# Four landing places for weight tiles and three more rows for gathered experts in a two-block transformer kernel

## What is computed

```python
# first block, last step: retrieval of single-neuron experts, 128 of them for each token
q = (xt @ w_query).reshape(t, PEER_HEADS, 2, PEER_KEY_DIM // 2)
s = jnp.einsum('thkd,hknd->thkn', q, sub_keys)
vals, idx = lax.top_k(s, PEER_TOPK)
cand = (vals[:, :, 0, :, None] + vals[:, :, 1, None, :]).reshape(t, PEER_HEADS, PEER_TOPK * PEER_TOPK)
best, pos = lax.top_k(cand, PEER_TOPK)
expert = i1 * N_SUB_KEYS + i2            # taken from idx at pos
gate = jax.nn.softmax(best, axis=-1)
a = jnp.einsum('cd,ced->ce', xb, u_tab[eb])
w = gb * jax.nn.gelu(a)
out = jnp.einsum('ce,ced->cd', w, v_tab[eb])
# second block, each of two layers
x = x + 0.5 * swiglu(rms_norm_2(x, ffn1_norm[l]), ffn1_w13[l], ffn1_w2[l])
x = x + (three gated attention branches) @ w_out[l]
x = x + 0.5 * swiglu(rms_norm_2(x, ffn2_norm[l]), ffn2_w13[l], ffn2_w2[l])
```

## Time and profile before

| | us |
|---|---|
| median of 3 runs | 4303.13 |
| lowest and highest | 4300.82, 4307.96 |
| the profiled execution | 4305.1 |
| its span, first to last instruction | 4303.3 |
| PE busy in the span | 3993.2 (93%) |
| POOL busy | 2348.1 (55%) |
| DVE busy | 2181.4 (51%) |
| ACT busy | 1402.0 (33%) |

### The profile page before, as it was taken

The page is one execution under the profiler, slowest core; times in us unless marked ns, Lnnn a source line. Parts: engine busy times, 40 slices in busy tenths (PEclk is TensorE's granted clock), DMA queues, the critical chain, the costliest instruction groups (busy, mean ns, idle before and its releaser), DMA issues.

```text
span 4303.3 us, 50720 instructions
## 1 busy us (share of the span) xinstructions
PE 3993.2 (93%) x17008; PEld 2839.7 (66%) x17008; DVE 2181.4 (51%) x4308; ACT 1402.0 (33%) x3024; POOL 2348.1 (55%) x3124
## 2 busy tenths in 40 slices
PE   9999988787887888988999999999999999999998
PEld 7877633333333555577867767888888867768887
DVE  8376877767776665543154544331332165534322
ACT  3142332222223444443223433332332133323222
POOL 7646543333334556656655456665665745546654
PEclk9999999999999999999999999999999999999999
DMA  5242899999999999944322212323223312213232
GB/s 148 86 106 79 349 427 427 427 427 427 427 412 387 394 369 367 411 134 132 98 69 74 64 60 83 103 96 99 94 97 95 98 54 69 77 49 108 94 97 82
DMA packets 187403, 828.07 MB, mean 192 GB/s; under 512 B 41360, under 2 KB 44096, under 8 KB 121664
## 3 DMA queue, kind: packets, MB, share of 16 engines
q0 software_dynamic: 73728, 536.90, 30.0%
q1 hardware_dynamic: 88448, 281.93, 20.6%
q10 hardware_dynamic: 25024, 6.69, 0.8%
HBM read 819.94 MB, written 4.59 MB: 192 GB/s over the span
## 4 chain that ended last, share of the span: by engine, by line
PE 67%; DMA 14%; DVE 9%; POOL 3%; issue 3%; ACT 2%; DVEq 1%; ACTq 0%; SPq 0%; POOLq 0%
PE bank L891 17%; PE bank L893 16%; PE bank L892 16%; PE bank L1290 7%; DMA rows_o<-in_peer_uv,of_picks_int 5%; DMA rows_x<-in_peer_uv,of_picks_int 3%; POOL wl L731 3%; DMA rows_w<-in_peer_uv,of_picks_int 2%; DMA raw<-in_w_l 2%; PE bank L985 1%; DVE rows_o L2696 1%; DMA work<-in_peer_uv,of_picks_int 1%; DVE rows_x L2696 1%; PE bank L1385 1%; PE bank L1517 1%
## 5 line engine op out<-in xcount | busy, mean ns | idle before, releaser
L731 POOL TENSOR_TENSOR wl<-raw,wh 128x256 fp32r<-128x256 f32 (+1 forms) x2064 | 1598.3, 805 | 598.0 <-ACT wh L1977 561.9
L891 PE MATMUL bank<-xh,wh 128*128 128x512 f32 (+1 forms) x2304 | 885.3, 384 | 27.8 <-POOL wl L731 27.0
L893 PE MATMUL bank<-xh,wl 128*128 128x512 f32 (+1 forms) x2304 | 863.9, 375 | 0.0
L892 PE MATMUL bank<-xl,wh 128*128 128x512 f32 (+1 forms) x2304 | 863.3, 375 | 0.0
L1977 ACT ACTIVATE wh<-raw 128x1024 fp32r<-128x1024 f32 x296 | 312.3, 1057 | 703.2 <-PE bank L893 491.2
L891 PEld LDWEIGHTS bank<-xh,wh 128*128 128x128 f32 x2304 | 435.4, 189 | 148.4 <-issue 40.1
L893 PEld LDWEIGHTS bank<-xh,wl 128*128 128x128 f32 x2304 | 435.4, 189 | 79.4
L892 PEld LDWEIGHTS bank<-xl,wh 128*128 128x128 f32 x2304 | 436.0, 189 | 74.3 <-issue 2.2
L1290 PE MATMUL bank<-rows_o,diag 128*128 128x512 f32 x768 | 374.4, 626 | 75.8 <-ACT diag L1934 75.1
L1290 PE MATMUL bank<-rows_x,diag 128*128 128x512 f32 x548 | 280.3, 645 | 62.5 <-ACT diag L1934 62.5
L2753 DVE TENSOR_TENSOR work<-bank,rstd 128x512 f32<-128x512 f32 (+1 forms) x176 | 108.5, 624 | 424.0 <-PE bank L893 421.6
(11 more groups left out here) (554 smaller groups left out, 7219.4 us busy)
## 6 DMA issues: line engine op xcount, KB each, us to landing
raw<-in_w_l SPq DMA_DIRECT2D x360, 512.0 KB
raw<-in_w_l SPq DMA_DIRECT2D x64, 448.0 KB
raw<-in_w SPq DMA_DIRECT2D x54, 512.0 KB
raw<-in_w_l SPq DMA_DIRECT2D x56, 256.0 KB
raw<-in_w SPq DMA_DIRECT2D x20, 256.0 KB
rows_o<-in_peer_uv,of_picks_int POOLq DMA_INDIRECT x192
raw<-in_uq_l SPq DMA_DIRECT2D x8, 384.0 KB
rows_x<-in_peer_uv,of_picks_int POOLq DMA_INDIRECT x137, 21.2
```

What stands on the lines that cost most here:

```text
L731: last = gp.tensor_tensor(wl[:, slot, c], raw[:, rslot, c], f32(wh[:, slot, c]), ALU.subtract)
L891: pe.matmul(out, wh[:, slot, c], ah, start=k == 0, stop=False)
L892: pe.matmul(out, wh[:, slot, c], al, start=False, stop=False)
L893: mm = pe.matmul(out, wl[:, slot, c], ah, start=False, stop=k == last)
```

## The change

1. `raw` gets two more places (`raw_more`) that are used from the fore tiles on: `raw_slot` and `raw_landed` say which place and which count of its semaphore a tile has. A load now waits for tile n-4 instead of n-2. The first four fore loads wait for the last pick that used place "raw" or "o3" (both before pick 350), where the first two waited for pick 342. The wait of the third up1 tile for pick 510 goes.
2. Row places: "o3" is given up after pick 350 (its memory holds `raw_more`); "norm" and "keys" come in its stead from 350, "temps" already from 390, "sums" takes over from "keys" at 425, and both "norm" and "sums" end at 456. So the last picks have 8 places (350 to 389), 9 (390 to 455) and 7 (456 to 511).
3. The searches of windows 3 to 15 are done earlier: four parts to a window in windows 5 to 10, instead of three, so that the last one is over in window 11 instead of 13. The scores for them come earlier too (`SCORES_AT`).
4. In the fore part ACT's high part comes one pick later (lag 3 instead of 2), DVE's reading of the products one pick later (4 instead of 3), and the multiplies and halves of a pair follow one pair later, so that DVE doesn't ask for a tanh that ACT has not made.

```diff
-RAWS = 2
+RAWS, RAW_SLOTS = 2, 4
+def raw_slot(glob):
+    return glob % (RAWS if glob < QUERY_END else RAW_SLOTS)
+def raw_landed(glob):
+    if glob < QUERY_END:
+        return 16 * (glob // RAWS + 1)
+    return 16 * ((QUERY_END // RAWS if raw_slot(glob) < RAWS else 0) + (glob - QUERY_END) // RAW_SLOTS + 1)
...
-        LAST_ROWS = ["o0", "o1", "o2", "o3", "x2", "x3", "late"]
-        TEMPS_FROM = 14 * WINDOW
+        LAST_ROWS = ["o0", "o1", "o2", "x2", "x3", "late"]
-        for rows, end in (..., (MIDDLE_ROWS, W_ROWS_TO), (LAST_ROWS, TEMPS_FROM), (LAST_ROWS + ["temps"], NB * PICKS)):
+        for rows, end in (..., (MIDDLE_ROWS, W_ROWS_TO), (LAST_ROWS + ["norm", "keys"], TEMPS_FROM),
+                          (LAST_ROWS + ["norm", "keys", "temps"], KEYS_TO), (LAST_ROWS + ["norm", "sums", "temps"], NORM_TO), (LAST_ROWS + ["temps"], NB * PICKS)):
...
+        SCORES_AT = {1: 4, 3: 5, 5: 6, 7: 7, 8: 8, 10: 9}
+        TOP_PLACES = [(q, g) for q in range(1, WINDOWS) for g in ((2, 4, 6, 7) if 5 <= q <= 10 else (2, 4, 6))]
+        TOP_AT = dict(zip(TOP_PLACES, [(w, part) for w in range(3, WINDOWS) for part in range(3)]))
...
             def load(n, l, source, nblk, extra=0):
-                if l is not None or n >= RAWS:
-                    sp.wait_ge(w_split.sem, w_split.at(n + 1 - RAWS, l, extra))
+                if glob < QUERY_END:
+                    if n >= RAWS:
+                        sp.wait_ge(w_split.sem, w_split.at(n + 1 - RAWS, None))
+                elif glob - RAW_SLOTS < QUERY_END:
+                    sp.wait_ge(p_mixed, RAW_MORE_FREE)
+                else:
+                    sp.wait_ge(w_split.sem, w_split.at(n + 1 - RAW_SLOTS, l, extra))
...
-            sp.wait_ge(p_mixed, W_ROWS_TO - 8)
...
-                            if up == "up1" and j == 2 and l == 0:
-                                sp.wait_ge(p_mixed, NB * PICKS - 2)
...
             def fetch(n):
+                elif row_of[n] == "norm":
+                    gp.wait_ge(x_turned, NB)
+                elif row_of[n] == "keys":
+                    gp.wait_ge(scored.sem, scored.at(HEADS1 * NB // 2 + 20, None))
+                elif row_of[n] == "sums":
+                    gp.wait_ge(p_mixed, KEYS_FREE)
+                    gp.wait_ge(p_turn, NB - 1)
...
-                if q % 2 == 1 and q + 3 < WINDOWS:
-                    sub_key_scores((q + 3) // 2 + 2)
+                if q in SCORES_AT:
+                    sub_key_scores(SCORES_AT[q])
...
-                for t in fore_slot_free(n, 2):
+                for t in fore_slot_free(n, 3):
                     fore_rounded(t)
                 for j in fore_at(n, 5):
                     if j % 2 == 0:
                         act.wait_ge(fore_read, j + 1)
                         act.activation(... ACT.Tanh, scale=0.5).then_inc(fore_tanh, 1)
+                        if j > 0:
+                            fore_high_half(j // 2 - 1)
-                    else:
-                        act.wait_ge(fore_mult, p + 1)
-                        act.activation(h_fore[:, 0, 0, p, :], ... ACT.Copy).then_inc(fore_hi, 1)
...
             def fore_gated(j):
                 if j % 2 == 0:
                     dve.tensor_tensor(a_, score[0][:, 0:FORE], fore_rstd, ALU.mult).then_inc(fore_read, 1)
-                    if p > 0:
-                        fore_rest(p - 1)
+                    if p > 1:
+                        fore_rest(p - 2)
+                    if p > 0:
+                        fore_product(p - 1)
...
-                        for j in fore_at(n, 3):
+                        for j in fore_at(n, 4):
                             fore_gated(j)
...
-                    elif q + 2 < WINDOWS:
-                        if g == 2:
-                            pick_keys(q + 2)
-                        if g == 4:
-                            pick_pairs(q + 2)
-                        if g == 6:
-                            pick_experts(q + 2)
+                    elif (q, g) in TOP_AT:
+                        w, part = TOP_AT[q, g]
+                        (pick_keys, pick_pairs, pick_experts)[part](w)
+            fore_product(FF - 1)
+            fore_rest(FF - 2)
             fore_rest(FF - 1)
```

More of the change, by code:

```diff
@@ L382, in build, with raw_of @@
         row_tiles = {**{f"{c}{b}": t[:, b, :] for c, t in (("o", rows_o), ("x", rows_x), ("w", rows_w)) for b in range(4)},
-                     "work": flat_row(work), "raw": flat_row(raw), "late": row_late[:], "spare": row_spare[:], "more": row_more[:], "temps": row_temps[:]}
+                     "work": flat_row(work), "raw": flat_row(raw), "late": row_late[:], "spare": row_spare[:], "more": row_more[:], "temps": row_temps[:], "norm": row_norm[:], "keys": row_keys[:], "sums": row_sums[:]}
+        def raw_of(glob):
+            slot = raw_slot(glob)
+            return raw[:, slot, :] if slot < RAWS else raw_more[:, slot - RAWS, :]
         RING_ROWS = ["o0", "o1", "o2", "o3", "work", "more", "w1", "w3", "w0", "w2", "x0", "x1", "x2", "x3"]
@@ L388, in build @@
         MIDDLE_ROWS = ["o0", "o1", "o2", "o3", "more", "w1", "w3", "w0", "w2", "x2", "x3"]
-        LAST_ROWS = ["o0", "o1", "o2", "o3", "x2", "x3", "late"]
-        TEMPS_FROM = 14 * WINDOW
+        LAST_ROWS = ["o0", "o1", "o2", "x2", "x3", "late"]
         row_of = list(FIRST_ROWS)
-        for rows, end in ((RING_ROWS, X_ROWS_TO), (MIDDLE_ROWS, W_ROWS_TO), (LAST_ROWS, TEMPS_FROM), (LAST_ROWS + ["temps"], NB * PICKS)):
+        for rows, end in ((RING_ROWS, X_ROWS_TO), (MIDDLE_ROWS, W_ROWS_TO), (LAST_ROWS + ["norm", "keys"], TEMPS_FROM),
+                          (LAST_ROWS + ["norm", "keys", "temps"], KEYS_TO), (LAST_ROWS + ["norm", "sums", "temps"], NORM_TO), (LAST_ROWS + ["temps"], NB * PICKS)):
             oldest = sorted(rows, key=lambda r: max([m for m, s in enumerate(row_of) if s == r], default=-1))
@@ L416, in sem @@
             return ctx.enter_context(nc.semaphore(name))
-        w_loaded = [sem(f"w_loaded{i}") for i in range(RAWS)]
+        w_loaded = [sem(f"w_loaded{i}") for i in range(RAW_SLOTS)]
         w_hi = sig("w_hi", 2 * FF, 2 * FFN_HI + sum(AT_L[s].tiles for s in HI_STAGES))
@@ L492, in build @@
         x_half_read = sem("x_half_read")
-        fetched = {r: sem(f"fetched_{r}") for r in FIRST_ROWS + ["temps"]}
+        fetched = {r: sem(f"fetched_{r}") for r in FIRST_ROWS + ["temps", "norm", "keys", "sums"]}
         fore_high = sem("fore_high")
@@ L1837, in high_query @@
                 act.wait_ge(product.sem, product.at(tile + 1 - RING, None))
-                act.wait_ge(w_loaded[tile % RAWS], 16 * (tile // RAWS + 1))
-                act.activation(wh[:, tile % RING, :], raw[:, tile % RAWS, :], ACT.Copy).then_inc(query_high, 1)
+                act.wait_ge(w_loaded[raw_slot(tile)], raw_landed(tile))
+                act.activation(wh[:, tile % RING, :], raw_of(tile), ACT.Copy).then_inc(query_high, 1)
             def gate_exp(q):
@@ L1875, in fore_rounded @@
                     act.wait_ge(product.sem, product.at(tile + 1 - RING, None))
-                act.wait_ge(w_loaded[tile % RAWS], 16 * (tile // RAWS + 1))
-                act.activation(wh[:, tile % RING, :], raw[:, tile % RAWS, :], ACT.Copy).then_inc(w_hi.sem, 1)
+                act.wait_ge(w_loaded[raw_slot(tile)], raw_landed(tile))
+                act.activation(wh[:, tile % RING, :], raw_of(tile), ACT.Copy).then_inc(w_hi.sem, 1)
             def fore_norm():
@@ L2655, in fore_gated @@
                 p = j // 2
-                a_, t_, h_ = (fore_work[:, 2 * m + p % 2, :] for m in range(3))
+                a_, h_ = fore_work[:, p % 2, :], fore_work[:, 4 + p % 2, :]
                 dve.wait_ge(product.sem, product.at(QUERY_END + j + 1, None))
```

71 lines of the change are left out of this document (42 added, 29 removed).

## The result

The changed kernel takes 4230.06 us (median, 4228.44 to 4231.07) against 4303.03 for the kernel before: a ratio of 0.9829, 95% interval 0.9811 to 0.9846, so 73 us or 1.7% faster. The forecast was 4236, range 4208 to 4268. The profiled execution has a span of 4229.3 us.

The account below looks back on a forecast made before the run. PE bound most of the kernel; waits for weight loads cost time in the picks and the ten iterations after. 4305.1 - 34 - 33 = 4238, less 2.0 from profiled execution to median: 4236 us, range 4208 to 4268.

Parts of the forecast that it names:

- (a): Picks: four landing places take ACT's 98.4 us of waits for weight tiles to nearly nothing, not all of it gain.
- the holes: Short, deep drops of the transfer rate below 427 GB/s in the picks; 52 us of transfers missing, 1200 to 1800 us.
- Rival A: Picks: rows or POOL, not ACT's wait, cause the holes; only 15 us come back, 4255 us, or 4274; chance 0.14.
- (b): Picks, the bound that remains: transfers bind at 2.88 us a pick, PE's floor is 2.70, 0.18 to spare.
- (c): Picks, row places: half of the 7 us hole at 1325 won; seven last places cost nothing, 38 us at worst.
- The hole of 1325: Picks, at 1325 us: 301 GB/s, 7 us lost, blamed on the move from 11 row places to 7 at pick 350.
- (d): Picks, earlier searches: cost 0 to 2 us in windows 9 and 10; gain is part of the holes that close.
- (e): Fore tiles in the picks: DVE's later reading of products costs nothing; bounds 0 and 0.5 us a tile.
- Rival C: Fore tiles: PE stops at each of 44 heads for DVE's reading; one whole pick each makes 4341 us; chance 0.04.
- (f): Picks: 15 of the 52 us of missing transfer time stay lost, so 37 come back.
- The iterations: Ten iterations after the picks: 15.2 us each, bound by loads into two places, fall to 11.9; gain 33 us.
- Rival B: Iterations after the picks: POOL and DVE slow each other; gain 25 to 15 us, 4244 to 4254 us; chance 0.13.

Follow-up runs that it names:

- the run in which POOL was never idle: The changed kernel with POOL making the low part of all four tiles of an iteration, DVE none; 4233.82 us.

## Why the prediction was right, point by point

The time, the two places of the gain and their sizes held: 34 + 33 = 67 us forecast, 32.5 + 35.5 + 6 = 74 measured in the two traces. The 6 lie where nothing was forecast, and the last mix varies by some 4 us between executions whose programs are the same up to it. Of the signs, two came short: 1400 to 1500 has 396 GB/s where 415 was asked for, and PE's wait for diag fell by 44%, not by half.

(a), ACT's wait. As an observation right: the wait vanished, and the places alone are enough for 26 of the 34 us. As the full cause of the holes wrong. The step failed where it read PE's 51.8 us and ACT's 98.4 us as one chain; the table shows the same 98 us of ACT's wait with nothing lost by it once DVE isn't tied to it (393.9 us with the wait, 394.3 without). DVE's own line in the earlier trace rows, 50.7 us for the tanh, was the one to follow. The size was right because it was not taken from that wait but from the transfers' shortfall, most of which any of the three parts gives back; in so far it was luck that the wrong chain did no harm. Rival A, another cause than this wait, was thus partly true, but its price, 15 us instead of 34, was not.

(b), the bound that remains. 2.88 us a pick by bytes against 2.70 by PE: the changed kernel had 2.87 in picks 456 to 480, and the run with half loads showed 2.70. Both held.

(c), rows. The hole of 1325 closed more fully than forecast, 413 GB/s, but no gain of time shows: the mix of pick 376 came at 1412.3, against 1410.3, and it lies at 1407.3 to 1409.4 in the three runs with the old searches and seven places. So the term of 3 to 5 us for this hole was mis-sized to that amount. Of the 7 us given back after pick 448, the kernel before gained some by catching up there: from a dot to its mix it took 6.7 us in picks 440 to 455 and 3.1 in 480 to 511, the changed one 3.2 and 2.6. The forecast's 2.5 us for two more tiles loaded before the last row are not seen: the run with two landing places takes the same 177.9 us from pick 448 to 511. How much is left for seven places in place of eight was not measured.

(d), searches. Put down as a part of the holes; in the table this part alone brings nearly all of the picks' gain (385.2 us for picks 376 to 511, against 418.7 before and 384.3 after). It was underrated most.

(e), the later reading. Taken at nothing, and it is nothing: no wait of PE's at lag 4, no loss at lag 5, 15 us at lag 7. Rival C's cliff, one pick a tile, does not appear up to lag 7; at lag 5 the time from a dot to its mix grows once, from 2.7 to 4.9 us (picks 456 to 480), and PE then keeps pace.

(f), what stays lost. 15 us forecast. By the earlier trace rows's columns after the change 1200 to 1500 lost 9 + 11 + 31 GB/s x 100 us and 1500 to 1700 4: 55 x 100 us / 427 = 13 us. Another 1.6 us are lost in 1100 to 1200, 420 GB/s where it was 427, inside the 0 to 2 us that (d) gave to windows 9 and 10.

A reading of the slices in the prediction is off, without weight in its sum: in the earlier trace rows, counted from 0, PE is under nine tenths in slices 5 to 15, 17 and 18, and the transfers stand at 427 GB/s in slices 5 to 10 only.

The iterations: 11.9 forecast, 11.7 measured, PE without a wait. Rival B's slowing is there in single instructions (below) but hidden: POOL had a little time left, 10.5 us of waits in 110. The Trainium skill's page "SBUF — State Buffer", section Who interferes with whom, says that a DVE instruction with two SBUF inputs contends with a GpSimd instruction that reads SBUF. The slower single instructions agree with it (POOL's pieces 0.998 us against 0.787, DVE's low part 1.483 against 1.226); whether the one waits for the whole of the other, as the page has it, no run here shows, and the time that the rival drew from it did not come. The 358 GB/s of the Trainium skill's page "DMA: Bandwidth & Descriptors", section Specifications, does not bind here: 425 over 300 us. (The prediction says that all of 1400 to 1800 before lay above it; 1600 to 1700, with 351, did not.)

## What to carry to other kernels

A long wait in a table of waits is not yet a cause: ask which engine has no time left in that stretch (busy plus waits for others near the whole, and never a wait for data), and count what that engine waits for. When several parts of a change seem to share a gain, undo them in pairs too; each alone can look worthless while together they are all of it. A size taken from the resource that will bind next (bytes over rate) held here although the chain that was blamed was the wrong one.

## What the runs showed of the hardware

A POOL piece of 128 x 256 with two inputs took 0.808 us on average into tiles from the two new places and 0.998 into those from the old, in the same iterations; with DVE's fourth tile left out, 0.792 and 0.787. So it isn't the place in memory but what DVE does beside. DVE's low part of a whole tile took 1483 ns where it had 1226 in the earlier trace rows. DVE's multiply of 256 columns took 585 ns on average in the changed kernel and 820 in the run in which POOL was never idle. The records of POOL's pieces overlap: mean 0.79 us, 0.75 from start to start.

A load of 512 KB took 3.5 us from its issue to its landing in the iterations and 7.7 (5.2 to 9.2) beside the gathers of the picks (medians of the run with four places and the old rest, 1860 to 1925 and 1440 to 1700 us).
